# One gated tile moved ahead of the short convolution, compact norm sums, early tables and unrolled programs in a one-core hybrid block

## The reference, cut to what matters

```python
h = layer_norm(x, ln_in_g, ln_in_b)
u_glu, z, xbc, dt_raw, gate_a, gate_b = split_in(h @ w_in)
# branch a: a gate, a depthwise convolution of 31 taps, a norm over the channels
a, g = jnp.split(u_glu, 2, axis=-1)
v = causal_dwconv(a * sigmoid(g), dw_w, dw_b)            # 31 taps, 1024 channels
y_a = silu(layer_norm(v, ln_g, ln_b)) @ w_conv_out
# branch b: a short convolution (4 taps), Mamba-2 heads in 4 groups, a norm per group
xbc = silu(causal_dwconv(xbc, conv_w, conv_b))           # 4 taps, 3072 channels
dt = softplus(dt_raw + dt_bias)
y = ssd_chunked(xs, dt, a_head, bm, cm) + xh * d_skip    # 32 heads
y_b = group_rmsnorm(y * silu(z)) * norm_w @ w_ssm_out
mix = (sigmoid(gate_a) * y_a + sigmoid(gate_b) * y_b) @ w_o
h = layer_norm(DN_ALPHA * h + mix, ln1_g, ln1_b)
h = layer_norm(DN_ALPHA * h + conv_ffn(h), ln2_g, ln2_b) # up, 3 taps, gate, down
# def layer_norm: (x - mean) * rsqrt(mean((x - mean)**2) + eps) * g + b, over the 1024 channels
```

## Time and profile before

| | |
|---|---|
| median of 3 runs | 2334.6 us |
| the profiled execution's own time | 2337.73 us |
| its span | 2335.9 us |
| mean granted clock of TensorE | 0.988 |
| PE busy | 2240.5 us (96%) |
| DVE busy | 1466.3 us (63%) |
| ACT busy | 1014.4 us (43%) |
| POOL busy | 82.2 us (4%) |
| moved by DMA | 207.74 MB, mean 89 GB/s |

### The profile page before, as it was taken

The page is one execution under the profiler, slowest core; times in us unless marked ns, Lnnn a source line. Parts: engine busy times, 40 slices in busy tenths (PEclk is TensorE's granted clock), DMA queues, the critical chain, the costliest instruction groups (busy, mean ns, idle before and its releaser), DMA issues.

```text
span 2335.9 us, 33115 instructions
## 1 busy us (share of the span) xinstructions
PE 2240.5 (96%) x12932; PEld 1951.8 (84%) x12932; DVE 1466.3 (63%) x1810; ACT 1014.4 (43%) x1429; POOL 82.2 (4%) x53
## 2 busy tenths in 40 slices
PE   7999999898999999999999999999999999999997
PEld 5787777676787788888899999999999889888886
DVE  6757888989965555654576676225358667732545
ACT  5546665653342555532536544223233465322331
POOL 0000010123000000000200000000000000000000
PEclk9999999999999999999999999999999999999998
DMA  4232223222222122233221122222223112223221
GB/s 155 82 110 82 92 99 103 95 72 72 90 90 90 55 101 96 91 124 144 80 106 37 55 91 90 91 90 90 91 73 107 59 38 84 97 90 106 92 90 54
DMA packets 35666, 207.74 MB, mean 89 GB/s; under 512 B 4930, under 2 KB 6978, under 8 KB 12132
## 3 DMA queue, kind: packets, MB, share of 16 engines
q1 hardware_dynamic: 29280, 194.66, 23.6%
q10 hardware_dynamic: 6276, 11.57, 1.7%
HBM read 204.05 MB, written 2.17 MB: 88 GB/s over the span
## 4 chain that ended last, share of the span: by engine, by line
PE 79%; DVE 12%; DVEq 4%; ACT 3%; issue 1%; ACTq 1%; DMA 0%
PE PS L515 25%; PE PS L517 24%; PE PS L519 24%; DVE vout L1861 4%; DVEq L1854 2%; PE PS L905 1%; DVE wlo L1632 1%; PE PS L931 1%; DVE hres L1730 1%; PE PS L615 1%; DVEq L1729 1%; PE PS L921 1%; ACT whi L1036 1%; DVE rstd L1662 1%; DVE zres L1728 0%
## 5 line engine op out<-in xcount | busy, mean ns | idle before, releaser
L515 PE MATMUL PS<-ahi,whi 128*128 128x512 f32 (+2 forms) x2376 | 736.2, 345 | 14.3 <-DVE xbc L1787 3.5
L517 PE MATMUL PS<-alo,whi 128*128 128x512 f32 (+2 forms) x2376 | 723.0, 339 | 0.0
L519 PE MATMUL PS<-ahi,wlo 128*128 128x512 f32 (+2 forms) x2376 | 721.9, 339 | 0.0
L1632 DVE TENSOR_TENSOR wlo<-raw,whi 128x2048 fp32r<-128x2048 f32 x174 | 398.4, 2290 | 466.4 <-ACT whi L1036 465.4
L1036 ACT ACTIVATE whi<-raw 128x2048 fp32r<-128x2048 f32 x168 | 321.7, 1915 | 644.5 <-PE PS L519 640.3
L515 PEld LDWEIGHTS PS<-ahi,whi 128*128 128x128 f32 x2376 | 416.0, 189 | 77.9 <-issue 28.8
L517 PEld LDWEIGHTS PS<-alo,whi 128*128 128x128 f32 x2376 | 415.4, 189 | 48.2 <-issue 1.7
L519 PEld LDWEIGHTS PS<-ahi,wlo 128*128 128x128 f32 x2376 | 415.0, 189 | 48.6
L515 PE MATMUL PS<-f2hi,whi 128*128 128x264 f32 (+2 forms) x800 | 215.2, 315 | 0.0
L517 PE MATMUL PS<-f2lo,whi 128*128 128x264 f32 (+2 forms) x800 | 215.1, 314 | 0.0
L519 PE MATMUL PS<-f2hi,wlo 128*128 128x264 f32 (+2 forms) x800 | 215.0, 314 | 0.0
(11 more groups left out here) (276 smaller groups left out, 2799.1 us busy)
## 6 DMA issues: line engine op xcount, KB each, us to landing
raw<-weights SPq DMA_DIRECT2D x181, 1024.0 KB, 4.8
acs_b<-acs_rows ACTq DMA_DIRECT2D x34, 256.0 KB, 3.3
const<-const ACTq DMA_DIRECT2D x2, 1232.0 KB, 5.6
x_in<-x_t SPq DMA_DIRECT2D x4, 512.0 KB, 5.1
out_t<-hres SPq DMA_DIRECT2D x16, 128.0 KB, 1.7
cols<-columns SPq DMA_DIRECT2D x1, 385.0 KB, 6.9
const<-const SPq DMA_DIRECT2D x1, 256.0 KB, 6.7
acs_rows<-dtt ACTq DMA_DIRECT2D x1, 64.0 KB
```

The lines of the kernel that those rows point to most:

```text
L515: nc.tensor.matmul(o, wh, h, start=first, stop=False)
L517: nc.tensor.matmul(o, wh, h, start=False, stop=False)
L519: mm = nc.tensor.matmul(out[j], wl, hi[j], start=False, stop=last)
L1632: v.tensor_tensor(wlo[s][:, :], raw[s][:, :], whi[s][:, :].bitcast(F32), ALU.subtract).then_inc(lo_ready, 1)
```

## The change

Five things change together.

1. **Order of the work.** The gate unit of tile 0 is taken out of group 0 and stands with `dt` ahead of `xbc`. The host's weight layout stays as it was (`PLAN`); a table `SOURCE` tells SP which unit to load at each turn, and `WORK` has the new stages. So SP's loads up to gate_b are written out instead of looped. In exchange each group g now makes the gated tiles 2g+1 and 2g+2, and the last has no second gate unit.
2. **Long taps.** Tile 0 gets 3 taps at the end of each `xbc` unit from the second on. Group g does tile 2g+1 (1, 3, 5, 7). In gate_b and ssm_out only tiles 2 and 4 are left for DVE, and tile 6 is the one shared with ACT and POOL.
3. **Compact sums.** The squares of a tile are summed by four matmuls of 128 columns (`chunk_sums`), each into 32 partitions, so that the root and the reciprocal run over 128x128. Four plain fp32 matmuls of 128x128 (`spread`) bring the result back to 128x512 in bank 5. They stand after 8 of the spin's turns, with 16 behind them (18 in LN2) in place of 30. In LN2 ACT copies the bank to SBUF (`ln_rows`). In gate_a `spread` stands between the two tiles of the last unit.
4. **Early tables.** `table(func)` is an activation over one column, whose table load comes at that place. In gate_a the last gate's sigmoids move behind all of the norm's outputs.
5. **Straight programs.** PE's and ACT's counted loops are written out: 9314 instead of 6494 rows on PE, 1176 instead of 1100 on ACT.

The diff, cut to its core:

```diff
-POOL_TILE = KD - 1
+POOL_TILE = KD - 2
+FIRST_TAPS = 3
+    ahead = [("dt", 1, 1, KD), ("glu0", 1, 2, KD), ("xbc", XBCT // 2, 2, KD), ("z_glu", 4 * GROUPS - 1, 2, KD)]
...
+            for u in range(2, WORK["gate_b"].u0 + 1):
+                sp.wait_ge(lo_ready, u - 1)
+                sp.dma_start(raw[u % 2][:, :], wstream[SOURCE[u]]).then_inc(raw_in[u % 2], 16)
...
-                    with pe.Fori(straight // 2, end // 2) as i:
+                    for i in range(straight // 2, end // 2):
                         for s in range(2):
                             unit(i, s)
...
+            def chunk_sums(squares, first, last):
+                for c in range(CHUNKS):
+                    mm = nc.tensor.matmul(PS[32 * c:32 * c + 32, 6 * 512:6 * 512 + P], ones[:, 0:32],
+                                          squares[:, c * P:(c + 1) * P], start=first, stop=last)
+                return mm
...
-                        nc.tensor.matmul(bank(6), ones, sq1[k % 2][:, :], start=(k == 0), stop=(k == KD - 1)
-                                         ).then_inc(n["pe"].sem, 1)
+                        chunk_sums(sq1[k % 2], k == 0, k == KD - 1).then_inc(n["pe"].sem, 1)
...
+            def spread(n, pe_odd=True):
+                after(pe, n["dve"], summed(pe_odd) + 1)
+                for c in range(CHUNKS):
+                    row = ident[:, 32 * c:32 * c + 1].to_broadcast([P, P])
+                    mm = nc.tensor.matmul(bank(5, P, c * P), row, rstd[:, 0:P], start=True, stop=True)
+                mm.then_inc(n["pe"].sem, 1)
...
-            spin(30)
+            spin(8)
+            spread(n_in)
+            spin(16)
...
-                z_glu(3, 0)
+                if g < GROUPS - 1:
+                    z_glu(3, 0)
...
+            def table(func):
+                nc.scalar.activation(next(scrap), ident[:, 0:1], func)
...
-                nc.scalar.activation(std[:, 0:T], bank(6), ACT.Sqrt, bias=col("eps5", 0), scale=1.0 / D
+                nc.scalar.activation(std[:, 0:P], bank(6, P), ACT.Sqrt, bias=col("eps5", 0), scale=1.0 / D
...
             act.wait_ge(params_in, 48)
+            table(ACT.Sqrt)
             ln_squares(n_in, x_in, {2: lambda: split_first(0), 4: lambda: split_first(1)})
...
             gate(stage, 2, ga)
+            table(ACT.Sqrt)
             ln_std(n_conv, False)
+            table(ACT.Silu)
             ln_out(n_conv, *conv_out, range(0, 4), False)
-            gate(stage, 3, ga)
+            split_next(stage, 1, 1)
             ln_out(n_conv, *conv_out, range(4, KD), False)
+            sigmoids(stage, 3, ga)
...
-              v.reciprocal(rstd[:, 0:T], std[:, 0:T])
-              drain()
+              v.reciprocal(rstd[:, 0:P], std[:, 0:P]).then_inc(n["dve"].sem, 1)
+              if rows is None:
+                  after(dve, n["pe"], KD + 2 if pe_odd else 3)
+                  rows = bank(5)
...
+                w = FIRST_TAPS * (2 * i + s - 1)
+                long_taps([0], max(w, 0), min(w + FIRST_TAPS, TAPS))
...
-                long_taps([2 * g], TAPS_AT[-1], TAPS)
-                low_next(stage, 2 * g + 1, 1)
-                glu(1)
+                long_taps([2 * g + 1], TAPS_AT[-1], TAPS)
+                if g < GROUPS - 1:
+                    low_next(stage, 2 * g + 1, 1)
+                    glu(1)
```

More of the change, by code:

```diff
@@ L95, with _source @@
 PLAN, UNITS = make_plan()
+WORK, _ = make_plan(True)
+def _source():
+    glu, z = [PLAN["z_glu"].u0 + 2 * j + j % 2 for j in range(KD)], [PLAN["z_glu"].u0 + 2 * j + 1 - j % 2 for j in range(KD)]
+    order = [0, glu[0], *range(1, PLAN["z_glu"].u0)]
+    for g in range(GROUPS):
+        order += [glu[2 * g + 1], z[2 * g], z[2 * g + 1], *glu[2 * g + 2:2 * g + 3]]
+    order += range(len(order), UNITS)
+    assert sorted(order) == list(range(UNITS))
+    return order
+SOURCE = _source()
 COLS = {}
@@ L423, in units @@
                 body(u // 2, u % 2)
-        def unit_loop(eng, stage, body, first=0, end=None):
-            end = stage.n if end is None else end
-            pairs = end // 2
-            if pairs > first // 2:
-                with eng.Fori(first // 2, pairs) as i:
-                    for s in range(2):
-                        body(i, s)
-            for u in range(2 * pairs, end):
-                body(u // 2, u % 2)
         @block.sync
@@ L697, in _ @@
                     tile(stage, ahi, alo, T, 1, 0, 0, [k])
-            tile(PLAN["xbc"], ahi, alo, T, 1, 0, 1, range(KD))
+            tile(WORK["glu0"], ahi, alo, T, 1, 0, 1, range(KD))
             def dt_tokens():
@@ L822, in _ @@
             variance(n_1)
-            spin(30)
-            linear(PLAN["ffn_up"], ahi, alo, T, ready=normed(n_1), together=4)
-            stage = PLAN["ffn_down"]
-            with pe.Fori(0, KD // 2) as i:
+            spin(8)
+            spread(n_1)
+            spin(16)
+            linear(WORK["ffn_up"], ahi, alo, T, ready=normed(n_1), together=4)
+            stage = WORK["ffn_down"]
+            for i in range(KD // 2):
                 for t in range(2):
@@ L843, in _ @@
             variance(n_2)
-            spin(30)
+            spin(8)
+            spread(n_2)
+            spin(18)
             for l, y in enumerate(layers):
-                stage = PLAN[f"in_{l}"]
+                stage = WORK[f"in_{l}"]
                 if l:
-                    down = PLAN[f"down1_{l - 1}"]
+                    down = WORK[f"down1_{l - 1}"]
                     first_units(stage, [wx[2], w2[stage.slot(1)]], y["n_pre"], every,
@@ L1042, in unit @@
                     body(i, s, stage.slot(s))
-                unit_loop(act, stage, unit, first, end)
+                units(stage, unit, first, end)
             def ln_squares(n, src, beside=None, pe_odd=True):
@@ L1125, in _ @@
                                  ).then_inc(psum_free[0], 1)
+            stage = WORK["glu0"]
+            split_next(stage, 0, 0)
+            nc.scalar.activation(sig[0][:, 0:T], bank(2 * stage.slot(0) + 1), ACT.Sigmoid).then_inc(sig_ok, 1)
             def dt_exponential():
@@ L1395, in _ @@
                 split_next(stage, 1, 1)
+                table(ACT.Exp)
                 after(act, y["v_ps"], 1)
@@ L1569, in _ @@
                         highs(0, s)
-                    with act.Fori(1, stage.n // 2) as i:
+                    for i in range(1, stage.n // 2):
                         for s in range(2):
@@ L1574, in _ @@
                             highs(i, s)
-                    stage = PLAN[f"down{h}_{l}"]
+                    stage = WORK[f"down{h}_{l}"]
                     if h == 0:
@@ L1644, in tap, with layer_norm @@
                 return v.scalar_tensor_tensor(acc[:, sh:n], ps[:, 0:n - sh], w, acc[:, sh:n], ALU.mult, ALU.add)
-            def layer_norm(n, src, hi, lo, each=None, pe_odd=True, units=(), late=None):
+            def layer_norm(n, src, hi, lo, each=None, pe_odd=True, units=(), late=None, rows=None):
                 after(dve, n["pe"], 1)
@@ L1773, in _, with long_taps @@
             low_at(2)
-            stage = PLAN["xbc"]
+            def long_taps(tiles, a, b, start=None):
+                for w in range(a, b) if start is None else [start + k for k in range(a, b)]:
+                    drain()
+                    for u in tiles:
+                        src, acc = cut(vpad, u * VW + w, T), cut(vout, u * T, T)
+                        wc = col("conv_w", u * TAPS + w)
+                        if isinstance(w, int) and w == 0:
+                            v.tensor_scalar(acc, src, wc, col("conv_b", u), ALU.mult, ALU.add)
+                        else:
+                            v.scalar_tensor_tensor(acc, src, wc, acc, ALU.mult, ALU.add)
+            stage = WORK["glu0"]
+            low_next(stage, 0, 0)
+            dve.wait_ge(sig_ok, 1)
+            v.tensor_tensor(vpad[:, TAPS - 1:TAPS - 1 + T], bank(2 * stage.slot(0)), sig[0][:, 0:T], ALU.mult
+                            ).then_inc(psum_free[stage.slot(0)], 1)
+            drain().then_inc(v_ok, 1)
+            stage = WORK["xbc"]
             def xbc_unit(i, s):
```

179 lines of the change are left out of this document (92 added, 87 removed).

## The result

| | before | changed |
|---|---|---|
| median | 2334.12 us (2333.4 to 2336.23, 4 runs) | 2319.44 us (2317.39 to 2321.93, 4 runs) |
| ratio | | 0.9931, 95% interval 0.9918 to 0.9945 |
| profiled execution, own time | 2337.73 | 2317.41 |
| span | 2335.9 | 2315.6 |
| PE busy | 2240.5 | 2223.0 |

The ratio is worth 16.1 us (12.8 to 19.1), the medians are 14.7 apart, the two profiled executions 20.3. The forecast was 17.4. The four times of the changed kernel lie in two pairs, 2317.4 and 2321.5 to 2321.9. Its profile is of the lower pair, and the profiled execution of the kernel before (2337.73) lies above its four times, so the two profiles show more of a gain than the medians do.

The account below looks back on a forecast made before the run. The prediction took PE's work plus PE's waits as the bound, with DVE binding ssm_out. Terms 8.5 + 3.5 - 14.5 - 1.0 - 12.2 - 1.7 = -17.4 took the median 2334.6 to 2317.2, said as 2317; range 2307 to 2329.

Parts of the forecast that it names:

- The moved unit: Tile 0's gate unit, moved ahead of xbc: +10.9 us there, group sums 3.0 earlier, 0.6 for low clock; sum +8.5.
- Tile 0's taps in xbc: In xbc: DVE falls behind at two later softplus pieces, giving PE two waits of about 1.5 us; +3.5.
- ssm_out: In ssm_out: fewer long taps on DVE shorten PE's waits for `wlo` and the low clock behind them; -14.5 us.
- the length that the prediction gave as a sign: ssm_out's 8 units in under 92 us would show the forecast right, still over 97 us wrong.
- gate_a and conv_out: There: waits of 0.61 and 0.93 us go, spread costs 0.9, the variance's matmul is 0.6 shorter; -1.0.
- The norms: LN_in, LN1 and LN2: short sums side by side, smaller root and reciprocal, earlier tables; -4.3, -4.0, -3.85, sum -12.2 us.
- rival A: In the norms: short sums run one behind another or wait for weights, giving -5 instead of -12.2; 2324 us, chance 0.14.
- ffn_up's table: In ffn_up: the written-out loop has no table load ahead of `whi`, in front of PE's 3.47 us wait; -1.3.
- Straight programs: PE's and ACT's loops written out: unrolling has nothing to give back, 0 us.
- Rival C: Across PE's program: each of 2820 new rows pays 0.012 us for code fetch, +34, so 2351 us; chance 0.08.
- Rival D: Across the loops: loop ends cost some 3 us unseen in records, and buffers cover softplus pieces; 2311 us, chance 0.15.
- rival B: In xbc, groups and ssm_out: DVE stays the bound in front, ssm_out gives only 10; about 2327 us, chance 0.16.

Follow-up runs that it names:

- e5: The kernel before with only PE's and ScalarE's counted loops written out: 2333.72 us, ratio 0.9987.
- e8: The changed kernel with the order of work and the long taps of before; compact sums, early tables and straight programs stay: 2322.54 us, ratio 0.9942.
- e9: The changed kernel with tile 0's taps kept away from the xbc units that carry a softplus piece: 2317.74 us, ratio 0.9919.
- e6: The changed kernel with the norms' sums, root and reciprocal over 128x512 again and no spread; early tables stay: 2326.67 us, ratio 0.9956.
- e11: The changed kernel with taps kept off softplus units, idle matmuls in four PE waits, 2 turns ahead of the spreads: 2310.28 us, ratio 0.9890.

## Why the prediction was right

The forecast was 2317 in a range of 2307 to 2329; measured are 2319.4, so 14.7 to 16.1 of the 17.4 came. That the sum is so close is in part luck: the norms gave less than forecast, the loops and their tables more, and by the stages of one profile the gain is 20.3. By its steps:

*The moved unit* (+10.9 in front, sums 3.0 earlier, 0.6 for the clock). dt to xbc grew by 13.5, of which by the count of matmuls 10.9 are the unit. The groups gave 3.7 against the old order with the same norms and programs; 3.0 of that are the `wlo` and the gate product that DVE no longer does ahead of the first copy. The 5.1 between the two profiles probably hold the low clock in the third group of the kernel before, since the two other profiles of the old order (e5, e8) have none in that group and take 270.0 and 270.6 instead of 272.1. PE's wait for `m_slot` grew to 6.04 and cost nothing, as the step had it: DVE goes through there at its own pace. The idle time lies elsewhere than forecast, though: 6.04 ahead of `m_slot` and 4.07 ahead of the group sums, where over 6 were named.

*Tile 0's taps in xbc* (+3.5). What dt to xbc grew beyond the unit is 2.3 to 2.6. The mechanism was half right: the second wait is the taps' (e9), the first is not; it was there before and the taps left it as it was.

*ssm_out* (-14.5). Between the profiles -15.5, against the old order -13.0 to -13.8. The first wait stayed at 3.03, forecast 3. All others for `wlo` inside the stage went. But the length that the prediction gave as a sign was wrong: it named under 92 us as right and over 97 as wrong, and measured are 98.3, after 113.8. It had counted 8 units of 10.9, the waits for `wlo` and the clock behind them, and had left out, among other things, that PE waits for `yn_lo` at the stage's start, 3.7 us before and 5.0 now. The gain was right, the level from which it was taken was not.

*gate_a and conv_out* (-1.0): -0.9. By the undone parts the order gives 1.0 there and the tables 0.6, and the compact sums cost 0.5 (95.83 with wide ones), as the step had put the price of the spread above the shorter sum.

*The norms* (-12.2). Here the step was right in its mechanism and too large in its size. At the full clock LN1 gave 4.2 and LN2 3.7, forecast 4.0 and 3.85. LN_in gave 1.5 to 3.0 instead of 4.3 (18.77 to 20.32 in the seven traces with compact sums and early tables and no turns among the sums, 21.80 before), and LN1 only 1.5 in the profiled run. In LN_in the first profile has 8 turns in 2.74 where 2.05 is the full clock's. What I left out is that shorter sums leave PE idle: the low clock comes into LN_in in every such trace and into LN1 in one, and the spins, which are there to keep PE busy, then stand in front of the spread at half speed. The undoing (e6) gives the net: 5.8 us for the compact sums by the ratios, 7.3 by the medians, where the stages at the full clock in LN1 say 9. One of the step's readings was wrong, without harm: the row x8 of 1.74 at the group sums is four matmuls, so 0.43 each and not 0.22, and the low clock from 457.7 lies over it. At the full clock (e11) the same four take 1.07, 0.27 each, so rival A's counter-argument stands.

*ffn_up's table* (-1.3): the wait went from 3.47 to 1.96, -1.5, and straight programs alone do it (e5). In the table this stage has 3.1, and the 1.6 beyond are the low clock that only the kernel before has there. *Straight programs* (0): they gave 2.5, this 1.5 among it. Rival C at 2351 is out; its 0.012 us a row was idle time beside other work. Rival D was half right: the loops did cost something, and the 1.5 that can be named are the table loads that they repeat, not their ends. What the rest is stays open. The prediction gave the rule behind rival D without its condition: the Trainium skill (Runtime: NRT & Kernel Launch, section Instruction fetch mechanics) speaks of a stall where the target of a taken branch isn't in the two pages that are held. No run here shows whether a loop of this kernel meets it.

*The rest of the difference between the profiles*, 2.1 us in the second block, is a low clock: before has one from 1819.7 to 1823.1, half of whose 3.4 us is lost; the profile after has none there, the second one of the same kernel has (1172.55 for 1171.10). It belongs to the run, not to the change. Such places, this one and ffn_up's, are part of why the profiles are 20.3 apart and the times 14.7 to 16.1.

The parts, undone one at a time, sum to 5.8 + 1.6 + 2.6 = 10.0 by the ratios, with 2.5 for the straight programs 12.5; the whole is 16.1. By the medians they are 7.3 + 3.1 + 3.1 + 2.5 = 16.0 of 16.8. Each interval is 5 to 8 us wide from end to end and those of the three undone parts overlap the changed kernel's, the one of the wide sums only at its end, so the signs of the tables and of the order rest on their stages in the traces. Every run with wide sums (2325.7 and more) lies above every run of the changed kernel (up to 2322.3). Rival A (2324) and rival B (2327) were wrong in their mechanism: the short sums did run side by side, and ssm_out was relieved in full.

## What to carry to other kernels

Where work on TensorE is made shorter inside a chain that other engines pace, look at the clock of that stretch before and after: its idle share rises, and the filler behind it may run at half speed in front of what it was to protect. A wait of 4.2 us at the start of a stretch was worth filling with idle matmuls (1.8 us there); one inside a stretch that DVE sets was worth nothing. Compare stages by several profiles of the same kernel before a step of 1.5 to 3 us is put down to an edit.
